# Late expert blocks of a two-layer encoder projected in pairs, with their cross products kept apart and added on VectorE

## The reference

```python
q = (xt @ w_q).reshape(T, 8, 2, 128)
s = einsum('thpd,pnd->thpn', q, sub_keys)         # 2 x 128 scores a head
sv, si = top_k(s, 16)                             # 16 best of each half
cand = sv[:, :, 0, :, None] + sv[:, :, 1, None, :]
cv, ci = top_k(cand.reshape(T, 8, 256), 16)       # 16 best pairs a head
experts = i1 * 128 + i2                           # 128 experts a token
gates = softmax(cv)
a = gelu(einsum('td,tkd->tk', x, u[experts])) * gates
y = einsum('tk,tkd->td', a, v[experts])
```

## Time and profile before

| | us |
|---|---|
| median of 3 timed runs | 1862.16 (1860.56 to 1862.18) |
| the profiled execution, whole | 1864.81 |
| its span, first to last instruction | 1863.0 |
| PE busy in it | 1811.3 (97%) |
| DVE busy | 1279.2 (69%) |
| ACT busy | 905.9 (49%) |
| POOL busy | 271.2 (15%) |

### The profile page before, as it was taken

The page is one execution under the profiler, slowest core; times in us unless marked ns, Lnnn a source line. Parts: engine busy times, 40 slices in busy tenths (PEclk is TensorE's granted clock), DMA queues, the critical chain, the costliest instruction groups (busy, mean ns, idle before and its releaser), DMA issues.

```text
span 1863.0 us, 31339 instructions
## 1 busy us (share of the span) xinstructions
PE 1811.3 (97%) x12212; PEld 1653.2 (89%) x12212; DVE 1279.2 (69%) x2402; ACT 905.9 (49%) x1526; POOL 271.2 (15%) x146
## 2 busy tenths in 40 slices
PE   7889999999999999999999999999999999999998
PEld 7779999999999888888787899999999988888886
DVE  6963984888955666665665559578898566666665
ACT  4555444544444445554534454444444444555553
POOL 6710845000000000000002228420000000000000
PEclk9999999999999999999999999999999999999999
DMA  7534454444456555567722345544444565555663
GB/s 248 174 125 158 160 167 162 158 159 159 159 172 207 194 195 194 194 204 255 256 75 80 124 148 183 169 156 155 157 157 159 183 210 195 192 192 192 216 216 100
DMA packets 89426, 324.10 MB, mean 174 GB/s; under 512 B 10048, under 2 KB 10560, under 8 KB 89152
## 3 DMA queue, kind: packets, MB, share of 16 engines
q1 hardware_dynamic: 85104, 307.42, 49.8%
q10 hardware_dynamic: 4176, 14.68, 2.4%
HBM read 321.01 MB, written 1.05 MB: 173 GB/s over the span
## 4 chain that ended last, share of the span: by engine, by line
PE 84%; DVE 7%; DMA 4%; ACT 2%; issue 2%; POOL 0%; SPq 0%; DVEq 0%; ACTq 0%
PE work L534 41%; PE y L582 34%; PE y L836 3%; DMA raw<-v 3%; PE y L562 2%; DVE y L1521 2%; PE work L711 1%; DVE low L443 1%; DVE far_homes L443 1%; PE y L809 1%; ACT far_homes L880 1%; ACT high L880 1%; DMA raw<-mla_in 0%; DMA raw<-conv_in 0%; PE y L758 0%
## 5 line engine op out<-in xcount | busy, mean ns | idle before, releaser
L880 ACT ACTIVATE high<-raw 128x1024 fp32r<-128x1024 f32 x472 | 496.9, 1054 | 492.9 <-PE work L534 437.4
L534 PE MATMUL work<-xT_high,high 128*128 128x256 f32 x2368 | 678.9, 287 | 14.4 <-POOL low L463 6.6
L534 PE MATMUL work<-xT_low,high 128*128 128x256 f32 x2368 | 671.3, 284 | 0.0
L534 PE MATMUL work<-xT_high,low 128*128 128x256 f32 x2368 | 671.1, 283 | 0.0
L443 DVE TENSOR_TENSOR low<-raw,high 128x1024 fp32r<-128x1024 f32 x385 | 470.9, 1225 | 253.1 <-ACT high L880 252.2
L534 PEld LDWEIGHTS work<-xT_high,high 128*128 128x128 f32 x2368 | 455.6, 192 | 17.2 <-ACT xT_high L927 8.6
L534 PEld LDWEIGHTS work<-xT_low,high 128*128 128x128 f32 x2368 | 455.8, 192 | 0.0
L534 PEld LDWEIGHTS work<-xT_high,low 128*128 128x128 f32 x2368 | 455.6, 192 | 0.0
L443 POOL TENSOR_TENSOR low<-raw,high 128x1024 fp32r<-128x1024 f32 x87 | 214.8, 2479 | 227.6 <-ACT high L880 227.5
L1140 ACT ACTIVATE xT_high<-big 128x256 fp32r<-128x256 f32 x256 | 105.2, 415 | 268.9 <-PE y L582 268.2
L582 PE MATMUL y<-high,xT_high 128*128 128x512 f32 x696 | 217.0, 392 | 2.2 <-DVE xT_low L1448 1.3
(11 more groups left out here) (197 smaller groups left out, 1491.1 us busy)
## 6 DMA issues: line engine op xcount, KB each, us to landing
raw<-u SPq DMA_DIRECT2D x256, 512.0 KB, 3.5
raw<-v SPq DMA_DIRECT2D x256, 512.0 KB, 4.3
raw<-wq SPq DMA_DIRECT2D x32, 512.0 KB, 3.5
raw<-conv_in SPq DMA_DIRECT2D x15, 512.0 KB, 4.8
aux<-ln_par ACTq DMA_DIRECT2D x9, 512.0 KB, 6.9
raw<-conv_out SPq DMA_DIRECT2D x8, 512.0 KB, 3.8
raw<-mla_out SPq DMA_DIRECT2D x8, 512.0 KB, 3.9
big<-diag ACTq DMA_DIRECT2D x6, 512.0 KB, 3.9
```

What stands on the lines that cost most here:

```text
L534: mm = nc.tensor.matmul(out_, w[:, cols], m[:, k, :], start=(k == 0 and n == 0), stop=(k == KD - 1 and n == 2))
L880: A(high_at(c), raw[:, slot, :], ACT.Copy).then_inc(high_made, 1)
```

## The change

- From block 35 on (`EARLY` = 35) blocks are projected two at a time, 46 pairs; block 127 stays alone. In `project_merged` the high weights meet both token parts in one matmul of 128 x 512 (the two parts now lie in one tile `xT`), and the low weights meet the high tokens in one of 128 x 256. That is 16 matmuls for a block where there were 24. The wide one leaves high x high in the left half of a PSUM bank and the cross product high x low in the right half.
- So there is a new sum: ACT copies the right halves of both banks to SBUF (`copy_cross`), DVE adds them to the left halves (`add_cross`), and only then ACT applies the gelu to both blocks at once (`gelu_pair`); `late` also handles both at once.
- A batch of gates follows each of the first 8 pairs and then two of every three (`PAIR_OF`), to pair 42.
- The choice is transposed behind block 30 (`CHOSEN_AT` = 31), where it was behind 39.
- POOL makes the low parts of blocks 3 to 28 and no more in this stage. DVE makes 29 and 30 within the choice, 31 and 32 right after it, and all later ones. The exponential stands ahead of the gelu of block 25.
- Blocks 9 to 34 have far homes too (3 of 6 blocks), and ACT rounds ahead of use as `last_high_u` says: after block n it rounds up to block n + 3 + n//6, from n = 18 on no further than 34.

```diff
@@
-EARLY = 40
-EXP_AT = 27
-PICK_LOWS = (25, 31)
+EARLY = 35
+PAIRS = (NKEYS - 1 - EARLY) // 2
+CHOSEN_AT = 31
+EXP_AT = 25
+PICK_LOWS = (29, 31)
...
-PER_BATCH = 2
+DENSE = 8
+PAIR_OF = [_b if _b < DENSE else DENSE + (_b - DENSE) * 3 // 2 for _b in range(BATCHES)]
+BATCH_OF = {_pair: _b for _b, _pair in enumerate(PAIR_OF)}
...
+U_FAR, U_FAR_FROM = (40, 48, 56), 9
+for _layer in range(DEPTH):
+    for _i in range(U_FAR_FROM, EARLY):
+        _k = (_i - U_FAR_FROM) % (len(U_FAR) + RING)
+        if _k < len(U_FAR):
+            far(f"u{_layer}", _i, U_FAR[_k])
...
+def last_high_u(n):
+
+    return max(n + RING, min(n + RING + n // 6, EARLY - 1)) if n >= 18 else n + RING + n // 6
...
                 low_stage(u0 + RING, u0 + PICK_LOWS[0])
-                low_stage(u0 + PICK_LOWS[1], u0 + EARLY + 4)
...
+            def project_merged(layer, pair):
+
+                first = FIRST[f"u{layer}"]
+                c0 = first + EARLY + 2 * pair
+                for c in (c0, c0 + 1):
+                    wait_low(c)
+                    if c == c0:
+                        pe.wait_ge(emptied, PROJECTED[f"u{layer}"] + c - first - 2)
+                    bank = bank_of(c - first)
+                    both = work[:, bank, :].rearrange("p (s t) -> p s t", s=2)
+                    w_high, w_low = high_at(c), low_at(c)
+                    for k in range(KD):
+                        cols = slice(k * P, (k + 1) * P)
+                        nc.tensor.matmul(both, w_high[:, cols], xT[:, :, k, :], start=(k == 0), stop=False)
+                        mm = nc.tensor.matmul(both[:, 0, :], w_low[:, cols], xT_high[:, k, :],
+                                              start=False, stop=(k == KD - 1))
+                    mm.then_inc(block_used, 1)
...
-                for c in range(u0 + EARLY, u0 + NKEYS):
-                    project_block(f"u{layer}", c, release=(c == u0 + NKEYS - 1))
-                    b, odd = divmod(c - u0 - EARLY, PER_BATCH)
-                    if odd and b < BATCHES:
-                        spread(b)
+                project(f"u{layer}", CHOSEN_AT, EARLY)
+                for pair in range(PAIRS):
+                    project_merged(layer, pair)
+                    if pair in BATCH_OF:
+                        spread(BATCH_OF[pair])
+                project_block(f"u{layer}", FIRST[f"u{layer}"] + NKEYS - 1, release=True)
...
+                def gelu_pair(pair):
+
+                    n, here = EARLY + 2 * pair, gated_tokens(pair)
+                    banks = work[:, pair_banks(pair)]
+                    act.wait_ge(sum_ok, PAIRS * layer + pair + 1)
                     if here < T:
-                        A(big[:, n, here:T], bank[:, here:T], ACT.Gelu)
-                    A(bank[:, 0:here], bank[:, 0:here], ACT.Gelu).then_inc(late_ok, 1)
+                        A(big[:, n:n + 2, here:T], banks[:, :, here:T], ACT.Gelu)
+                    A(banks[:, :, 0:here], banks[:, :, 0:here], ACT.Gelu).then_inc(late_ok, 1)
+
+                def copy_cross(pair):
+
+                    A(cross[:], work[:, pair_banks(pair), T:2 * T], ACT.Copy).then_inc(cross_ok, 1)
...
                     gelu(n)
                     if n + 1 < EARLY:
-                        split_after(u0 + n + 1)
+                        act.wait_ge(block_used, u0 + n + 2)
+                        highs_to(u0 + last_high_u(n + 1))
...
+                for pair in range(PAIRS):
+                    n = u0 + EARLY + 2 * pair
+                    act.wait_ge(block_used, n + 2)
+                    copy_cross(pair)
+                    make_high(n + 1 + RING)
+                    if pair in BATCH_OF:
+                        place(BATCH_OF[pair])
+                    gelu_pair(pair)
+                    if pair + 1 < PAIRS:
+                        split_after(n + 2)
...
+            def add_cross(layer, pair):
+
+                dve.wait_ge(cross_ok, PAIRS * layer + pair + 1)
+                sums = work[:, pair_banks(pair), 0:T]
+                V.tensor_tensor(sums, sums, cross[:], ALU.add).then_inc(sum_ok, 1)
...
+                for pair in range(PAIRS):
+                    n, b = EARLY + 2 * pair, BATCH_OF.get(pair)
+                    more = b is not None and b + 2 < BATCHES
+                    add_cross(layer, pair)
                     make_low(dve, V, u0 + n + 4)
-                    gate(layer, b)
-                    late(layer, n)
-                    late(layer, n + 1)
-                    if b + 2 < BATCHES:
+                    if b is not None:
+                        gate(layer, b)
+                    late(layer, pair)
+                    if more:
                         make_onehots(layer, b + 2)
-                    make_low(dve, V, u0 + n + 5)
-                    if b + 2 < BATCHES:
+                    if pair + 1 < PAIRS:
+                        make_low(dve, V, u0 + n + 5)
+                    if more:
                         scale_onehots(layer, b + 2)
```

More of the change, by code:

```diff
@@ L64 @@
 BATCHES = T // BATCH
-PER_BATCH = 2
+DENSE = 8
+PAIR_OF = [_b if _b < DENSE else DENSE + (_b - DENSE) * 3 // 2 for _b in range(BATCHES)]
+BATCH_OF = {_pair: _b for _b, _pair in enumerate(PAIR_OF)}
 GATE_SCALE = 2.0 ** 15
-assert EARLY + PER_BATCH * BATCHES <= NKEYS
+assert EARLY + 2 * PAIRS == NKEYS - 1 and PAIR_OF[-1] < PAIRS
 OUT_HIGHS = (0, 1, 2, 3, 4, 5, 7, 8)
@@ L154, in last_high, with pair_banks, gated_tokens @@
     return c + RING + max(0, n - GROW_FROM + 1) // GROW_EVERY
+def last_high_u(n):
+    return max(n + RING, min(n + RING + n // 6, EARLY - 1)) if n >= 18 else n + RING + n // 6
 def bank_of(n):
     return (n + RING) % BANKS
-def gated_tokens(n):
-    return min(T, BATCH * ((n - EARLY) // PER_BATCH + 1))
+def pair_banks(pair):
+    first = bank_of(EARLY + 2 * pair)
+    return slice(first, first + 2)
+def gated_tokens(pair):
+    return BATCH * sum(p <= pair for p in PAIR_OF)
 def program(nc, x_rows, x_cols, positions, conv_par, diag, mla_par, ln_par, keys, w_uq, w_uk, w_uv,
@@ L510, in project_block @@
                     out_ = work[:, bank_of(c - first), 0:T]
-                    if c >= first + BANKS:
+                    if c == first + NKEYS - 1:
+                        pe.wait_ge(emptied, PROJECTED[name] + c - first - 2)
+                    elif c >= first + BANKS:
                         pe.wait_ge(emptied, c - BANKS + 1 - first + PROJECTED[name])
@@ L813, in _ @@
                             mm.then_inc(score_mm, 1)
-                project(f"u{layer}", 1, EARLY)
+                project(f"u{layer}", 1, CHOSEN_AT)
                 pe.wait_ge(chosen_ok, layer + 1)
@@ L1123, in place @@
                 def place(b):
-                    done = EARLY + PER_BATCH * b
+                    done = EARLY + 2 * PAIR_OF[b]
                     act.wait_ge(spread_ok, batches_before(layer) + b + 1)
@@ L1128, in place @@
                       ACT.Copy, scale=1.0 / GATE_SCALE).then_inc(placed, 1)
-                for n in range(EARLY, NKEYS - 1):
-                    gelu(n)
-                    b, odd = divmod(n - EARLY, PER_BATCH)
-                    if odd and b < BATCHES:
-                        place(b)
-                    if n + 1 < NKEYS - 1:
-                        split_after(u0 + n + 1)
+                for pair in range(PAIRS):
[8 more added lines that the diff above has]
+                        split_after(n + 2)
                 v0 = FIRST[f"v{layer}"]
@@ L1160, in _ @@
                 split_after(u0 + NKEYS - 1)
-                gelu(NKEYS - 1)
+                last = work[:, bank_of(NKEYS - 1), 0:T]
+                A(last, last, ACT.Gelu).then_inc(late_ok, 1)
                 ln_rows(2 * layer + 1)
@@ L1453, in combine @@
                 make_low(dve, V, v0 + RING - 1)
-                late(layer, NKEYS - 1)
+                late_last(layer)
                 done = v0 + RING
```

49 lines of the change are left out of this document (23 added, 26 removed).

## The result

The changed kernel takes 1868.24 us, the median of 9 runs (1864.51 to 1871.05). The kernel before takes 1861.22 beside it (9 runs, 1859.09 to 1862.64). The ratio is 1.0032 with a 95% interval of 1.0023 to 1.0041: 6.0 us slower by the ratio and 7.0 by the medians, where 5.5 us faster was forecast. The profiled execution of the changed kernel took 1867.16 us, its span is 1865.4; before it was 1864.81 and 1863.0.

What follows compares the result with a forecast made beforehand. PE, busy 97%, was taken as the bound, with its waits. 19.3 + 16.0 - 28.8 - 1.0 = 5.5 us gained, 1862.2 to 1856.7, given as 1856.5; 8 in 10 range 1841 to 1869, own range 1850 to 1862.

Steps and rivals of the forecast that it cites:

- the new wait: PE before block 29 in each layer, waiting for block 25's gelu: 12.7 us late, 14.4 with the slow clock.
- The lookup: DVE step L1331 in the choice, expected to start about 5.5 us later, at about 256.9, because POOL holds DVE.
- The removed wait for the one-hot rows: PE behind the transposes: early transposes remove the wait and slow stretch, 2.7 + 1.7 and 2.7 + 1.5 us.
- Part 2: Whether ACT and DVE keep up in the pairs: costed at nothing, with 2 us to spare on the banks.
- the merged products: Late blocks in pairs: a slice falls from 360.1 to 346.9 ns, 19.3 us gained in all.
- signs of being wrong: PE waiting in pair after pair, wide matmuls above 227 ns, or block 29 late by under 8 us.
- the long wait: Before block 29: 12.7 us late plus 1.7 of slow clock a layer, 28.8 us lost in all.
- the waits removed: Around the choice: waits for one-hot rows, slow stretches and lateness of 4.0 and 3.4 us go, 16.0 us in all.
- The short wait: Rival: POOL leaves DVE's last steps alone, block 29 is 7.2 us late, 1845.5 us; chance 0.25.
- DVE as the bound: Rival: in pairs with a batch DVE needs 0.5 us more than PE, 1880 us, at half 1868.5; chance 0.12.
- The wide matmul saves nothing: Rival: in the pairs a wide matmul carries the overhead of two, 19.3 us lost, 1876 us; chance 0.05.
- Part 1: The merged products' term: 13.1 ns less a slice, 19.3 us in all, against the skill page's 2.5 ns issue gap.

Runs made afterwards that it cites:

- e1: Changed kernel with ACT rounding ahead no further than block 31, so blocks 32 and up are rounded behind the exponential: 1850.82 us, ratio 0.9940.
- e3: As e1, but POOL stops at block 24 and DVE makes the low parts of blocks 25 to 30 within the choice: 1841.65 us, ratio 0.9888.
- e9: The kernel before with only the transposes of the choice moved, behind block 30 instead of block 39: 1854.67 us, ratio 0.9962.
- e8: e4 with the merge undone: three products of 256 columns a slice, no copy or add of cross products: 1851.14 us, ratio 0.9937.
- e6: e4 with the two token parts side by side, so a wide product reads one stretch: 1841.24 us, ratio 0.9884.
- e7: e4 with the narrow product summed into the bank half that holds the other cross product: 1842.28 us, ratio 0.9897.
- e11: e4 with the order of wide and narrow products turned in every second slice: 1838.77 us, ratio 0.9872.
- e12: e4 with narrow before wide from the second slice of each block on: 1836.25 us, ratio 0.9867.
- e4: As e1, but DVE makes low parts 29 to 32 within the choice and the choice is transposed behind block 32: 1841.72 us, ratio 0.9897.

## Why the prediction was wrong

**The parts that held.** The place and the mechanism of the new wait were as forecast: the gelu of block 25 behind the rounding of block 32 on ACT, that behind a slot which DVE frees late, and DVE late since POOL's subtractions hold its small steps. The lookup was put at 256.9 and came at 256.43; block 29 was put 12.7 us late and came 13.4 and 13.55 late. That these lie so close is in part luck. Block 28's low part was put at 253.9 (its terms, 202.7 + 48.4 + 2.4, make 253.5) and ended at 255.05, and of the eight steps that were to stand behind it, 3.05 us, only two did, 1.4 us. Counted from block 1, which began 1.1 us earlier than before, the lookup is 6.1 us later and not 5.5, which is most of what block 29 is later than forecast. e1 took away the first link and e3 the last, and each gave what the link was worth. The removed wait for the one-hot rows was put at 2.7 + 1.7 and 2.7 + 1.5 us, 8.6 in all; e9 gained 7 us by the times (interval 4.7 to 9.7), and its stretch from block 1's row to the v blocks is 4.36 us shorter in the first layer and 4.06 in the second, 8.4 in all. The pairs keep up, as Part 2 said: PE waits for no bank. The v blocks begin after 1.05 us of waiting, 0.4 more than before, where 0.5 was put.

**The step that failed is the first term of the sum, the merged products.** The prediction took a slice as the sum of two lengths from unmixed rows, 226.9 + 120.0 = 346.9 ns, and gave the full 13.1 ns a slice, 19.3 us. The low value does exist (346.7), but about three quarters of the slices have 353.3. The mean of 351.7 saves 8.4 ns, 12.4 us: 6.9 us less than forecast; e8 puts the whole merge at 11.3. The prediction had said that no row shows wide and narrow taking turns, bounded the gain between 0 and 19.3, and then took its upper end. It had a reason only for the two lengths by themselves, none for the turn. Of its signs of being wrong this is the one that came: the wide matmuls take more than 227 ns, 232 to 241 at the higher value.

**A smaller part of it is the cost of the long wait.** 12.7 + 1.7 a layer was forecast. Measured are 13.4 + 2.7 and, in the second layer, 13.55 + 2.6: 3.4 us more over both. The 1.7 came from a wait of 2.7 us; behind the one of 12.7 the clock was at 1.2 GHz for nearly 6 us.

**The sum again.** Forecast for both stages 5.5 us gained; 6.9 and 3.4 off make 4.8 lost, and the two profiles show 4.8 lost. So exact a match is chance: e8's 11.3 would take off another us, and the waits removed were about half a us more than forecast (8.4 for the one-hot rows, 4.1 and 3.9 up to the transposes, 16.4 in all against 16.0). The interval of the times is 4.3 to 7.6, so they agree with 4.8; the further 1 to 2 us of ratio and medians are not told apart from scatter. The profiled execution of before lay 3.6 us above its median of 9 and that of after 1.1 below, so the profile pair alone would have shown a loss of 2.4.

**The rivals.** The short wait was not it (POOL does hold DVE). DVE as the bound was not it: near the last batches DVE has idle moments of 0.6 and 1.1 us and PE waits for nothing. "The wide matmul saves nothing" was wrong as a mechanism, though its direction was right: a third of the saving was lost, not all. The forecast's own range of 1850 to 1862 had no room for both terms going the same way; the wider one, to 1869, just has. One slip in Part 1 changes nothing: 2.5 ns is a fifth of the 13.3, not a sixth.

**What stays open.** Why the alternation has two values, and why it keeps the one it begins with. The layout (e6), the bank half (e7) and the number of changes (e11, e12) are excluded; with e12's order the alternation has the lower value throughout, but whether that comes from its phase or from the two equal neighbours in each block is not told apart. What tells one start from another, no run here shows.

## What to carry to other kernels

An operation's length in a row of its like is a bound, not a price, for its length in a mix; where a term rests on a mix that no row shows, take less than the bound, and let the range hold the term at well under it (here 11.3 to 12.4 came of 19.3). When a table of order is changed, follow each in-order engine's list for an entry that waits for something late and has something urgent behind it: here one entry cost 17 us, and moving it made 1850.8 out of 1868.2. And when an idle engine is given more work, look at which engine's short steps it stands beside: taking four subtractions from POOL (e3) was worth as much as moving DVE's low parts and the transposes (e4).

## What the runs showed of the hardware

- Matmuls of 512 and 256 columns in turns, each with its own weights, run at one of two rates, 346.7 or 353.3 ns for the two at a granted clock of 1.00, fixed for a whole stretch; the slower is a pattern of three (350, 361, 349). In unmixed rows they are 226.9 and 120.0. With the order turned from the second slice on (e12) the alternation has the lower rate everywhere, worth 4.8 us in 1840.
- Some of DVE's small steps of 0.28 and 0.43 us take 2.5 to 2.6 us when they meet POOL's subtraction of 128 x 1024 (2.4 us): one of them passes between two of POOL's. Without POOL the same ones take 0.29 and 0.42 (e3). The Trainium skill ("SBUF — State Buffer", section "SBUF: two separate sides") says that the two engines share one pair of ports, as an exclusive lock for a whole instruction, and not for every kind of DVE step; this case agrees: the subtraction's 2.4 us is the length that a held step shows.
- After 12.7 us without a matmul two blocks took 2.7 us more than at the full clock, with 1.2 GHz granted for nearly 6 us; after 2.7 us without one it was 1.7 us.
